# Hybrid mixers with routed experts on one core: two expert pieces loaded in the first mixer, combinations on four banks, ranks from two comparisons

## The reference

```python
def hier_moe(h, w_group, b_group, w_router, b_router, w_gate, w_up, w_down):
    g_idx = jnp.argmax(g_logits, axis=-1)
    e_logits = jnp.take_along_axis(e_logits, g_idx[:, None, None], axis=1)[:, 0]
    top_val, top_idx = lax.top_k(e_logits, TOP_K)
    weights = jax.nn.softmax(top_val, axis=-1) * g_prob
...
    for e in range(N_EXPERTS):
        hid = jax.nn.silu(hf @ w_gate[e]) * (hf @ w_up[e])
        y = y + (hid @ w_down[e]) * combine[:, e:e + 1]
```

## Time and profile before

| | us |
|---|---|
| three runs | 773.81, 775.25, 775.29; median 775.25 |
| the profiled execution | 774.62 |
| its span, first to last instruction | 772.5 |
| PE busy | 719.3 (93%) |
| DVE busy | 324.5 (42%) |
| ACT busy | 207.0 (27%) |
| moved by DMA | 241.62 MB |

### The profile page before, as it was taken

How to read it: one execution, slowest core, us unless ns; L and a number is a source line. 1 busy time by engine, 2 the same in 40 slices (tenths; PEclk the granted TensorE clock), 3 DMA queues, 4 the chain that set the end, 5 groups by cost and what they waited for, 6 DMA issues and landing times.

```text
span 772.5 us, 16726 instructions
## 1 busy us (share of the span) xinstructions
PE 719.3 (93%) x7452; PEld 458.6 (59%) x7452; DVE 324.5 (42%) x688; ACT 207.0 (27%) x416; POOL 31.8 (4%) x99
## 2 busy tenths in 40 slices
PE   8999999999989998999999999999998997786895
PEld 7778787648655564555547745785764454343442
DVE  7476886624363323333137053633355231221222
ACT  2574568316100000000033263540330000000104
POOL 7006000000000000000000000000000000000000
PEclk9999999999999999899999999999999999998999
DMA  8644113399999999999999814518799999999995
GB/s 262 208 94 157 57 57 112 120 417 418 385 421 417 422 420 421 420 420 420 414 350 370 260 51 168 209 58 335 317 365 420 420 420 419 421 421 421 420 406 196
DMA packets 73863, 241.62 MB, mean 313 GB/s; under 512 B 10103, under 2 KB 37869, under 8 KB 54718
## 3 DMA queue, kind: packets, MB, share of 16 engines
q1 hardware_dynamic: 73582, 240.00, 79.8%
q10 hardware_dynamic: 208, 0.54, 0.2%
HBM read 239.48 MB, written 1.05 MB: 311 GB/s over the span
## 4 chain that ended last, share of the span: by engine, by line
PE 67%; DMA 17%; DVE 6%; SPq 4%; ACT 3%; issue 2%; PEld 0%; PEldq 0%; ACTq 0%
PE ps L1940 10%; PE ps L1611 10%; PE ps L1138 9%; DMA M<-in_m_w_gate_dram 7%; PE ps L1445 7%; PE ps L1547 6%; DMA M<-in_m_w_down_dram 5%; PE ps L1697 4%; DMA M<-in_m_w_up_dram 4%; PE ps L1562 4%; SPq L512 2%; DVE H L2555 1%; SPq L506 1%; DMA M<-in_e_w_in_dram 1%; PE ps L1084 1%
## 5 line engine op out<-in xcount | busy, mean ns | idle before, releaser
L1611 PE MATMUL ps<-M 128*32 128x256 f32 x2000 | 125.0, 398 | 15.5 <-DMA M<-in_m_w_gate_dram 10.2
L1611 PEld LDWEIGHTS ps<-M 128*32 128x32 f32 x2000 | 66.0, 114 | 72.2 <-issue 16.4
L1138 PE MATMUL ps<-M 128*128 128x272 f32 x352 | 85.3, 397 | 0.1
L1940 PE MATMUL ps<-M 128*128 128x256 f32 (+2 forms) x288 | 79.9, 434 | 0.0
L1547 PEld LDWEIGHTS ps<-M 128*128 128x128 f32 x608 | 71.5, 192 | 12.2 <-issue 11.7
L1547 PE MATMUL ps<-M 128*128 128x128 f32 x608 | 76.9, 278 | 0.0
L1138 PEld LDWEIGHTS ps<-M 128*128 128x128 f32 x352 | 65.6, 190 | 15.5 <-issue 1.7
L1940 PEld LDWEIGHTS ps<-M 128*128 128x128 f32 x288 | 53.7, 190 | 22.6 <-issue 15.6
L1562 PE MATMUL ps<-M 128*128 128x512 f32 (+1 forms) x120 | 60.7, 627 | 5.4 <-DVE H L2555 5.4
L1697 PE MATMUL ps<-M 128*32 128x512 f32 x448 | 55.9, 644 | 9.6 <-DMA M<-in_m_w_down_dram 9.6
L2552 DVE TENSOR_TENSOR H<-H,ps 128x512 f32<-128x512 f32 x60 | 41.3, 688 | 53.2 <-PE ps L1562 53.0
(11 more groups left out here) (466 smaller groups left out, 856.6 us busy)
## 6 DMA issues: line engine op xcount, KB each, us to landing
M<-in_m_w_gate_dram SPq DMA_DIRECT2D x28, 2048.0 KB, 17.9
M<-in_m_w_up_dram SPq DMA_DIRECT2D x22, 2048.0 KB, 21.0
M<-in_m_w_down_dram SPq DMA_DIRECT2D x21, 2048.0 KB, 22.2
M<-in_m_w_down_dram SPq DMA_DIRECT2D x14, 1024.0 KB, 16.7
M<-in_o_w_in_dram SPq DMA_DIRECT2D x12, 1024.0 KB, 9.3
M<-in_e_w_in_dram SPq DMA_DIRECT2D x11, 1024.0 KB, 5.9
M<-in_m_w_up_dram SPq DMA_DIRECT2D x9, 1024.0 KB, 18.6
M<-in_m_w_gate_dram SPq DMA_DIRECT2D x9, 1024.0 KB, 8.6
```

The source lines that it names most:

```text
L1138: ins = pe.matmul(ps[:, n % 4, 0:T], wringE[:, (n // 2) % 4, k, (n % 2) * P:(n % 2) * P + P], (xnE if n else xuE)[:, k], start=(k == 0), s ...
L1611: ins = pe.matmul(ps[32 * e:32 * e + 32, 3 * x, 0:FF], xgT[q % 2][:, k, 32 * e:32 * e + 32], w, start=(k == 0), stop=(k == KD - 1))
L1940: ins = pe.matmul(ps[rows, unit % 4, 0:n], lhs(k), rhs(k), start=(k == 0), stop=(k == KD - 1))
```

## The change

Three parts:

- **Loads.** Of unit 2 (the first down, slot 3) experts 1 and the first half of 2, and of unit 4 the piece `set_aside(1)`, together 2 MiB, are sent as soon as the fourth doubling's `y_done` and the second `lru_in` are there; the rest of unit 2 (2.5 MiB) at its old place. Unit 2 becomes five loads instead of two (three more issues). `set_aside(0)` stays at unit 1.
- **Banks.** Combination `j` goes to `COMBINE_BANK[j]`, that is banks 6, 7, 4, 5, 6, and PE waits for `acc` only at the fifth (which exists in layer 0 alone).
- **Ranks.** `chosen_two` compares each of an expert's seven earlier neighbours with >= and its seven later ones with > (the eight logits lie in a padded row `EP`, padding -3e38) and sums the 14 results; mask and difference are gone. The two comparisons do not wait for each other. `EP` is set once a layer.

```diff
 GATHER_BANK = [1, 4, 5, 2]
+COMBINE_BANK = [6, 7, 4, 5, 6]
...
                 if y == 0:
+                    sp.wait_ge(s("y_done"), 4)
+                    sp.wait_ge(s("lru_in"), 2)
+                    sp.dma_start(slots[3][:, 1, :], down[:, 1, :]).then_inc(s("ld_gn_e2"), 16)
+                    sp.dma_start(slots[3][:, 2, 0:D], down[:, 2, 0:D]).then_inc(s("ld_gn_e2"), 16)
+                    set_aside(1)
                     sp.wait_ge(s("sa_evac"), NC)
                     sp.wait_ge(s("lru_in"), 6)
-                    whole(2, down[:, 0:4])
+                    sp.dma_start(slots[3][:, 2, D:2 * D], down[:, 2, D:2 * D]).then_inc(s("ld_gn_e2"), 16)
+                    for e in (0, 3):
+                        sp.dma_start(slots[3][:, e, :], down[:, e, :]).then_inc(s("ld_s3"), 16)
...
                         but_quarters(u, up[:, 0:4], "ld_pv_ys")
-                        for e in range(2):
-                            set_aside(e)
+                        set_aside(0)
                         continue
...
-                    bank = 6 + j % 2
+                    bank = COMBINE_BANK[j]
...
-                        if j >= 2:
-                            pe.wait_ge(s("acc"), acc0 + nu * q + j - 1)
+                        if j >= 4:
+                            pe.wait_ge(s("acc"), acc0 + nu * q + j - 3)
...
+                v.memset(EP, -3.0e38)
...
-                    link(tt(GE[:, t_], el[:, t_].unsqueeze(2).to_broadcast([P, m, 8, 8]), el[:, t_].unsqueeze(3).to_broadcast([P, m, 8, 8]),
-                            ALU.is_ge))
-                    link(tt(GE[:, t_], GE[:, t_], low[:, :, :].unsqueeze(1).to_broadcast([P, m, 8, 8]), ALU.mult))
-                    link(tt(DF[:, t_], GE[:, t_], GE[:, t_].rearrange("p t b a -> p t a b"), ALU.subtract))
-                    link(v.tensor_reduce(rk[:, t_], DF[:, t_], AXX, ALU.add))
+                    own = el[:, t_].unsqueeze(3).to_broadcast([P, m, 8, 7])
+                    for x, op in ((0, ALU.is_ge), (1, ALU.is_gt)):
+                        others = EP[:, t_, 8 * x:8 * x + 8]
+                        others = bass.AP(others.tensor, others.offset, [list(d) for d in others.ap] + [[1, 7]])
+                        ins = tt(BT[:, t_, :, 7 * x:7 * x + 7], others, own, op)
+                    link(ins)
+                    link(v.tensor_reduce(rk[:, t_], BT[:, t_], AXX, ALU.add))
```

More of the change, by code:

```diff
@@ L61 @@
 FIRST_LAYER = [UNIT_SLOT[0][:NU - 1].count(j) for j in range(4)]
-ALONE = {0: ("ld_x0_e2", 16 + 64), 1: ("ld_x1_e2", 16 + 112), 2: ("ld_x2_e2", 16 + 48), 5: ("ld_gn_e2", 64 + 64), 8: ("ld_lora", 112 + 64)}
+ALONE = {0: ("ld_x0_e2", 16 + 64), 1: ("ld_x1_e2", 16 + 112), 2: ("ld_x2_e2", 16 + 48), 5: ("ld_gn_e2", 64 + 48 + 64), 8: ("ld_lora", 112 + 64)}
 for _u in range(NU):
@@ L138, in program @@
         rkc = sb("rkc", [P, 2, 8])
-        low = sb("low", [P, 8, 8])
         ones_h = sb("ones_h", [P, P], BF16)
@@ L282, in program @@
         pe4 = rt(3, NG, 8)
-        el, rk, A8, oh1, oh2, s8 = (rt(3, 8) for _ in range(6))
-        GE, DF = rt(3, 8, 8), rt(3, 8, 8)
+        rk, A8, oh1, oh2, s8 = (rt(3, 8) for _ in range(5))
+        EP, BT = rt(3, 22), rt(3, 8, 14)
+        el = EP[:, :, 7:15]
         AA = rt(48).bitcast(BF16).rearrange("p (t e) -> p t e", t=3)
@@ L1587, in loaded @@
                         pe.wait_ge(s("ld_pv_ys"), 304)
+                    elif y == 0 and u == 2:
+                        pe.wait_ge(s("ld_gn_e2"), 64 + 48)
                     elif y == 0 and u == 3:
@@ L1747, in experts @@
                                 for j in range(nu):
-                                    if j >= 2:
-                                        pe.wait_ge(s(f"ov_acc{y}"), i1 * nu + (j - 1 - nu))
+                                    if j >= 4:
+                                        pe.wait_ge(s(f"ov_acc{y}"), i1 * nu + (j - 3 - nu))
                                     combine(j, RT[0][0:CAP], yst[0][0:CAP]).then_inc(s(f"ov_cb{y}"), 1)
@@ L2186, in _ @@
             eight = iota[:, 0:8]
-            tt(low[:, :, :], eight.unsqueeze(1).to_broadcast([P, 8, 8]), eight.unsqueeze(2).to_broadcast([P, 8, 8]), ALU.is_lt)
-            v.tensor_scalar(rkc[:, 0], eight, -6.0, None, ALU.add)
-            v.tensor_scalar(rkc[:, 1], eight, -7.0, None, ALU.add)
+            v.memset(rkc[:, 0], 1.0)
+            v.memset(rkc[:, 1], 0.0)
             v.tensor_copy(ones_h[:, :], ones[:, :])
@@ L2551, in accumulate @@
                         c = slice(512 * hf, 512 * hf + 512)
-                        return tt(H[:, n, c], H[:, n, c], ps[:, 6 + j % 2, :], ALU.add)
+                        return tt(H[:, n, c], H[:, n, c], ps[:, COMBINE_BANK[j], :], ALU.add)
                     for g in range(4):
                         c = slice(256 * g, 256 * g + 256)
-                        ins = tt(H[0:META, 2, c], H[0:META, 2, c], ps[32 * g:32 * g + META, 6 + j % 2, 0:256], ALU.add)
+                        ins = tt(H[0:META, 2, c], H[0:META, 2, c], ps[32 * g:32 * g + META, COMBINE_BANK[j], 0:256], ALU.add)
                     return ins
```

## The result

The changed kernel takes 779.43 us (median of 20 runs, 775.90 to 783.02) beside 775.69 us of the kernel before (20 runs, 773.81 to 779.12). The profiled execution took 779.00 (span 777.3), against 774.62 (span 772.5).

What follows compares the result with a forecast made beforehand. The DMA stream of layer 0's expert weights was taken as the bound up to 391.88. Loads -0.2, banks 0 and ranks -0.1 sum to -0.3: 774.95 us from a median of 775.25, range 773.2 to 777.0.

Steps and rivals of the forecast that it cites:

- into a stretch with 56 GB/s: First mixer, 127.00 to 147.25: early loads go out while DMA carries little; expected -0.2 us, bounds 0 to -1.2.
- three rivals: Stream up to 5.0 us earlier, chance 0.13; clock falling in the last wait, 0.13; ranks fully on the path, 0.06.
- the slower one: Layer 0's last expert units: clock falls in the last wait, +1.0 or +2.7 us; chance 0.13.
- Part 1's gain: Early loads, judged by what was still queued at 195.69 in the routing: -0.2 us, 0 to -1.2.
- the 5.0 us lead: Queue starting at 147.25 is shorter by 2.10 MB, 5.0 us at most; 0.2 taken to show at 195.69.
- Part 2: Layer 0's combinations: each turn 0.88 us shorter, 6.2 in seven, all absorbed by waits for loads: 0; layer 1 gains 0.
- Rival 2: Layer 0's last units: longer waits let the clock fall, +1.0 us (776.3) or +2.7 (778.0); chance 0.13.
- Part 3: Ranks in layer 0's late routing: steps save at most 0.27 us, mostly hidden behind the early gather: -0.1; layer 1: 0.

Runs made afterwards that it cites:

- e2: Changed kernel with the early loads undone, banks and ranks alone: 774.66 us against 775.79 for the kernel before, ratio 0.9990.
- e8: The changed kernel traced a second time, nothing altered: 778.59 us, one run.
- e9: Kernel before with the new banks of the combinations alone: 775.35 us against 776.48, ratio 1.0000.
- e1: Kernel before with the 2 MiB of early loads alone, banks and ranks as before: 781.03 us against 775.79, ratio 1.0063.
- e4: Kernel before with the 2 MiB of early loads sent 6 us later, behind the second chunk: 780.18 us against 775.79, ratio 1.0063.
- e5: Changed banks and ranks, only unit 4's 512 KB early, ahead of the last output-weights load: 776.56 us against 775.84 (kernel before), ratio 1.0007.
- e6: Changed kernel with all 2 MiB sent ahead of the last load of output weights: 779.88 us against 775.84 for the kernel before, ratio 1.0048.
- e11: Kernel before with 512 KB of unit 2 early, four loads, one behind each of the first four chunks: 777.64 us against 776.57, ratio 1.0014.
- e3: Kernel before with only the 512 KB piece of unit 4 sent early: 778.83 us against 775.79, ratio 1.0046.
- e7: Kernel before with 512 KB of unit 2 sent early at once, as four loads with 1 KB rows: 780.15 us against 775.84, ratio 1.0062.

## Why the prediction was wrong

**The step that failed** is the sentence that part 1 goes "into a stretch with 56 GB/s" and can bring 0 to -1.2: its bounds excluded a loss. The row that it rests on says that the DMA is nearly idle there (share 0.18), and I took that for a free resource. But it is not unused. The same row counts 708 matmuls and 711 weight loads in 20.25 us, and their code comes by DMA too (q8 of the profile), one packet of 16 KB about every 4 us. With the loads of 2 MiB on the way such a packet comes late, by about 2 us, and TensorE stands until it is there. None of the three rivals has this mechanism; the slower one put the fall of the clock into layer 0's last units. The sign was in the trace of before: 0.29 us of idle time that ends with "issue" at 133.55, behind a packet of code. It tells that the code comes with nothing to spare, and not that a load is in its way: e2 has 0.50 of such time at 145.42, with no load from 131.6 to 148.8. The row of e2:

```profile
145.42 0.30 PE L1382 MATMUL ps<-M,K 128*32 128x64 f32 x4 [0.50 <-issue]
```

I had counted what waits for data, not what an engine waits for when no one releases it.

The Trainium skill (Runtime: NRT & Kernel Launch, Instruction fetch mechanics) says that each engine streams its code in blocks of 16 KiB by DMA and that this is mostly hidden. The packets agree in size; where a load stood in front, 1.78 to 2.7 us were not hidden. The Trainium skill (DMA: Bandwidth & Descriptors, Queues, rings and completion order) also has each DMA engine go round its queues packet by packet; that would bear on how long code stands behind weights, but no run here shows the order inside an engine.

**Part 1's gain** was rightly put at next to nothing. SP's issue behind the last chunk comes 150.82 - 147.25 = 3.57 later, and PE's last wait of layer 0 ends 395.38 - 391.88 = 3.50 later; in e8 it is 2.02 and 393.83 - 391.88 = 1.95. So 0.07 us of the 5.0 us lead are left, with the ranks' share in it, where 0.2 was forecast for the lead alone. e2, which has no early loads, makes up 0.18 on the same way (147.91 and 392.36, that is 0.66 and 0.48 late), so nothing of the lead can be told. From 150.80 to 195.69 the DMA moved only 371 GB/s in the changed kernel (401 before, from 147.25): the queue ran dry in the routing.

**Part 2** went where it was forecast to go, but its size was wrong. A turn of layer 0 is 1.22 us shorter and not 0.88 (from the first combination of 512 columns to the up matmuls behind the last, for instance 243.66 to 247.29, before 241.40 to 246.25), in seven times 8.5 and not 6.2. The waits that take the saving, in the changed kernel before units 18 to 22:

```profile
355.22 3.66 PE L1620 MATMUL ps<-M 128*32 128x256 f32 x64 [2.00 <-DMA M<-in_m_w_gate_dram]
...
365.16 3.66 PE L1620 MATMUL ps<-M 128*32 128x256 f32 x64 [2.22 <-DMA M<-in_m_w_up_dram]
...
375.30 3.64 PE L1706 MATMUL ps<-M 128*32 128x512 f32 x32 [2.69 <-DMA M<-in_m_w_down_dram]
...
385.16 3.66 PE L1620 MATMUL ps<-M 128*32 128x256 f32 x64 [1.63 <-DMA M<-in_m_w_gate_dram]
...
395.38 1.93 PE L1620 MATMUL ps<-M 128*32 128x256 f32 x32 [0.42 <-DMA M<-in_m_w_up_dram]
```

Busy 60.7 - 55.7 = 5.0 us and 5.4 us of idle time are gone from the group (1.3 of the 5.0 are layer 1's, which was to gain 0: its eight matmuls take 3.70 and not 3.89), and unit 22 still waits 0.42. Rival 2 was right that such waits bring half clock (e9) and wrong that this reaches the end. Its condition, a wait of about 2 us, doesn't decide: behind the waits of 2.00 to 2.69 above the units take 3.64 and 3.66, as at full clock, behind 2.60 in e9 5.34.

**Part 3**: VectorE's steps and TensorE's early gather in the changed kernel:

```profile
193.26 0.34 DVE L2461 TENSOR_TENSOR M<-M 128x56 f32<-128x56 f32 x2
193.64 0.27 DVE L2463 TENSOR_REDUCE M<-M 128x8 f32<-128x112 f32 x1
193.94 0.17 DVE L2464 TENSOR_TENSOR M<-M,rkc 128x8 f32<-128x8 f32 x1
```

```profile
192.03 2.92 PE L1467 MATMUL ps<-M 128*128 128x128 f32 x24 [0.29 <-DVE M L2483]
194.78 0.29 PE L1460 MATMUL ps<-M,ones_h 128*128 128x32 bf16 x2
```

The 1.08 us became 193.94 - 193.26 = 0.68, a saving of 0.40 where I allowed at most 0.27: the two comparisons together take 0.34. On the path it is worth less: from the gather's start to the ranks there are 2.75 us, before 191.28 - 188.46 = 2.82. That is 0.07, forecast 0.1.

**The sum of what happened**, in the profiled executions: -0.58 at 126 (the runs differ by as much before any change acts, and this is no part of it), the stall 2.14 - 0.29 = +1.85, the fall of the clock +2.6 (TensorE is 143.69 - 139.83 = 3.86 behind after it, from +1.27 at 133.55), -0.29 up to SP's issue behind the last chunk (3.86 to 3.57; not taken apart), the lead and the ranks together -0.07, and +1.3 in layer 1 from 395 on, in all 4.8 of span.

**What stays open.** The +1.3 of layer 1 has half clock in its last turns, for instance here in the changed kernel, behind a wait for ScalarE (32 matmuls otherwise take 3.64):

```profile
734.87 2.53 PE L1091 MATMUL ps<-ones 128*128 128x512 f32 x4 [1.18 <-ACT M L891]
737.34 4.73 PE L1706 MATMUL ps<-M 128*32 128x512 f32 x32
```

Such falls stand in layer 1 of each trace, at other places each time, and the runs of one kernel spread over 3 to 9 us. Whether the later start of layer 1 has any part in it was not settled; e8 is 2.0 late at the start of layer 0's loads and 4.4 at the end. e1, e4, e5, e6 and e11 also have half clock in the routing of layer 0, e5 and e11 without a stall ahead of it, so it doesn't hang on the stall. That the code packet stands behind the weights inside the DMA engines, and isn't asked for later, was not seen directly: the trace has a packet's beginning, not its request, and not its engine. The 4.1 us in e4, against 1.1 to 1.6 elsewhere, speak for it. What is shown is that the stall comes with the loads, goes with them (e2), moves with them (e4), ends behind a packet of code each time, and is absent where 512 KB flow between two packets (e5) or a little at a time beside them (e11). No version beat both kernels by what can be measured; e2, banks and ranks alone, has the lowest median, 774.66, not told from the kernel before.

## What to carry to other kernels

A stretch in which the DMA is idle is free for bulk loads only if the engines' own code doesn't need it: look at how many instructions an engine gets through per us there, at the times of the code's packets (the queue of kind "instruction"), and for idle time that already ends with "issue". Keep early loads out of these packets' way: 512 KB in the stretch of large matmuls ahead gave no stall here (e5), in pieces of 128 KB behind each chunk 0.68 us at most (e11), at once among the small matmuls 1.8 to 2.2. Earlier alone is not enough: in e6 the loads pushed the output weights in front of the code. And a saving on an engine that waits for a saturated stream stays a wait, even if the clock falls in it.

## What the runs showed of the hardware that I had not expected

Between 512 KB and 2 MiB the stall hardly grows with the bytes: 512 KB gave stalls of 1.78 (e3) and 2.18 (e7), 2 MiB 2.14 to 2.7 (the changed kernel, e1, e4, e6, e8), though the 2 MiB kept the queue full for some 10 us. Each of these traces has one stall of that size and not one per packet of code: the packet behind the late one came in time (1.1 us after TensorE went on in the changed kernel and in e1, 1.5 in e8), at half clock and at full, though weights still flowed until 137 to 139. Why the one packet is late and the next is not, no run here shows.
